# A last down projection with the tokens in rows: the final two token tiles of a decoder step on one Trainium2 core

## The reference

```
h2 = x * (1 + sc2) + sh2
ua, ub = jnp.split(h2 @ w_up, 2, axis=-1)
uc, ffn_conv_new = causal_dwconv(ua, ffn_conv_prev, w_ffn_conv, b_ffn_conv)
ffn = (jax.nn.gelu(uc) * ub) @ w_down
x = layer_norm(DN_ALPHA * x + g2 * ffn, ln2_g, ln2_b)
```

## Time and profile before

| | |
|---|---|
| median of 3 runs | 1551.62 us (1549.88 to 1554.25) |
| profiled execution, its own time | 1554.13 us |
| span of the profiled execution | 1552.5 us |
| TensorE busy | 1462.7 us (94%) |
| VectorE busy | 837.4 us (54%) |
| ScalarE busy | 404.1 us (26%) |
| GpSimd busy | 78.2 us (5%) |
| mean granted TensorE clock | 0.978 of full |

### The profile page before, as it was taken

How to read it: one execution, slowest core, us unless ns; L and a number is a source line. 1 busy time by engine, 2 the same in 40 slices (tenths; PEclk the granted TensorE clock), 3 DMA queues, 4 the chain that set the end, 5 groups by cost and what they waited for, 6 DMA issues and landing times.

```text
span 1552.5 us, 25588 instructions
## 1 busy us (share of the span) xinstructions
PE 1462.7 (94%) x9800; PEld 1312.1 (85%) x9800; DVE 837.4 (54%) x1273; ACT 404.1 (26%) x729; POOL 78.2 (5%) x111
## 2 busy tenths in 40 slices
PE   6999999799998999599899999999999999999996
PEld 3878787566565877499899999999999999999996
DVE  3306787994555564644754544445444454544566
ACT  2212434353544575624341210010000000010011
POOL 0333000000000000002210000000000000000013
PEclk9899999999999999899999999999999999999998
DMA  9865863763872111431211111111112111111122
GB/s 342 261 216 163 236 189 102 223 188 122 271 227 90 34 38 45 171 110 41 69 41 41 39 39 58 55 41 48 33 41 68 41 44 34 58 55 41 34 78 96
DMA packets 178111, 159.99 MB, mean 103 GB/s; under 512 B 12267, under 2 KB 158327, under 8 KB 178018
## 3 DMA queue, kind: packets, MB, share of 16 engines
q1 hardware_dynamic: 145412, 141.15, 28.7%
q10 hardware_dynamic: 30566, 17.50, 3.9%
q0 software_dynamic: 2048, 0.20, 0.2%
HBM read 142.25 MB, written 13.79 MB: 101 GB/s over the span
## 4 chain that ended last, share of the span: by engine, by line
PE 80%; DVE 10%; issue 3%; ACT 3%; SPq 2%; DMA 2%; ACTq 0%; DVEq 0%
PE ps L2185 43%; PE ps L1933 13%; PE ps L2136 5%; PE ps L2016 3%; PE ps L1994 3%; PE ps L2297 2%; PE ps L2034 2%; DVE stick L945 1%; PE ps L2048 1%; PE ps L1856 1%; DVE k_page L855 1%; PE ps L2236 1%; DVE pr L924 1%; SPq L610 1%; DVE pr L949 1%
## 5 line engine op out<-in xcount | busy, mean ns | idle before, releaser
L2185 PE MATMUL ps<-acts_lo,w_hi 128*128 128x344 f32 x1008 | 213.9, 320 | 0.0
L2185 PE MATMUL ps<-acts_hi,w_hi 128*128 128x344 f32 x1008 | 213.8, 320 | 0.0
L2185 PE MATMUL ps<-acts_hi,w_lo 128*128 128x344 f32 x1008 | 212.8, 319 | 0.0
L1933 PE MATMUL ps<-acts_hi,w_hi 128*128 128x344 f32 (+1 forms) x552 | 186.1, 337 | 6.5 <-DVE w_lo L813 2.9
L1160 DVE CAST w_hi<-w_raw 128x1024 fp32r<-128x1024 f32 x72 | 49.7, 690 | 239.4 <-PE ps L2185 227.7
L1933 PE MATMUL ps<-acts_lo,w_hi 128*128 128x344 f32 (+1 forms) x552 | 178.8, 324 | 0.0
L1933 PE MATMUL ps<-acts_hi,w_lo 128*128 128x344 f32 (+1 forms) x552 | 178.8, 324 | 0.0
L2185 PEld LDWEIGHTS ps<-acts_lo,w_hi 128*128 128x128 f32 x1008 | 170.6, 189 | 0.0
L2185 PEld LDWEIGHTS ps<-acts_hi,w_hi 128*128 128x128 f32 x1008 | 169.7, 188 | 0.0
L2185 PEld LDWEIGHTS ps<-acts_hi,w_lo 128*128 128x128 f32 x1008 | 167.9, 188 | 0.0
L1933 PEld LDWEIGHTS ps<-acts_hi,w_hi 128*128 128x128 f32 (+1 forms) x552 | 103.9, 188 | 24.1 <-issue 16.6
(11 more groups left out here) (334 smaller groups left out, 2398.1 us busy)
## 6 DMA issues: line engine op xcount, KB each, us to landing
w_ada<-in_w_ada SPq DMA_DIRECT2D x12, 2048.0 KB, 8.9
w_raw<-in_w_up SPq DMA_DIRECT2D x44, 512.0 KB, 3.8
k_page<-in_cache_fox_k SPq DMA_DIRECT2D x64, 192.0 KB, 3.0
k_page<-in_cache_sb_k SPq DMA_DIRECT2D x64, 192.0 KB, 2.9
k_page<-in_cache_fox_v SPq DMA_DIRECT2D x64, 192.0 KB, 2.9
k_page<-in_cache_sb_v SPq DMA_DIRECT2D x64, 192.0 KB, 3.6
w_raw<-in_w_in ACTq DMA_DIRECT2D x15, 512.0 KB, 5.5
w_raw<-in_w_down SPq DMA_DIRECT2D x16, 384.0 KB, 3.4
```

The source lines that it names most:

```text
L1933: last = nc.tensor.matmul(bank[0:cols, 0:CH], w[:, n % 2, k, 0:cols], a[:, k, c * CH:(c + 1) * CH], start=k == 0 and w is w_hi and a is ac ...
L2185: last = nc.tensor.matmul(proj_ps[half][:, c, 0:CH], w[:, half, k], a[:, k, c * CH:(c + 1) * CH], start=k == 0 and w is w_hi and a is hi, ...
```

## The change

Tiles 3 and 4 (n = 7, 8) no longer get their part of the last down projection with the features in partitions. In last_mms the tokens of the tile are the stationary operand (g_hi, g_lo: 128 x 128) and the weights the moving one, 512 columns wide, so that the product has the tokens in partitions and 512 features in columns; there are two halves for each tile, each of 5 x 3 products. No turn follows.

What this needs is made in the first span: side_rows turns, after m = 2, 4 and 6, the gate (one column of modT, repeated 128 times) into gate_rows, and resT of tiles 3 and 4, which lacks only the last group, into res_rows; ScalarE evicts all three (128 x 1024 each). ScalarE also copies the weights of the first two output tiles into the wide buffers wd_hi and wd_lo (four copies, w_c), since the moving operand is read from there.

In the new last_half VectorE multiplies the product by gate_rows, adds it to res_rows and takes the statistics of the half, in three instructions of 512 columns. norm_last now works on res_rows and writes the last instruction of tile 4 in two halves, each of which SyncE stores by itself.

The order on the engines is new: TensorE runs half 0 of tile 3, the turns of tiles 0 and 1, half 1 of tile 3, the turns of tile 2 and the two halves of tile 4. VectorE runs last_half(0, 0), norm2 of tiles 0 and 1, last_half(0, 1), norm2 of tile 2, norm_last(0), the two halves of tile 4 and norm_last(1). scale2 stays with VectorE for tiles 5, 6 and 7; for the sampled tokens and tiles 0, 1 and 2 GpSimd does the multiply by ln2g ahead of its addition of ln2b. SyncE stores tile 3 ahead of tile 2.

```diff
@@ gpsimd
-                pool.wait_ge(y_g, n + 1)
+                if n < Y_ROWS_DVE:
+                    pool.wait_ge(y_g, n + 1)
+                else:
+                    pool.wait_ge(y_n, n + 1)
+                    nc.gpsimd.tensor_tensor(y_tile[n % 3][0:rows], y_tile[n % 3][0:rows], ln2g[0:rows], ALU.mult).then_inc(y_g, 1)
+                    pool.wait_ge(y_g, n + 1)
                 nc.gpsimd.tensor_tensor(y_tile[n % 3][0:rows], y_tile[n % 3][0:rows], ln2b[0:rows], ALU.add).then_inc(y_o, 1)
@@ vector
+            def last_half(j, half):
+
+                dve.wait_ge(o_pm, D_AT + 2 * KT + 2 * j + half + 1)
+                at = Z_DONE * j + 3 * half
+                v = res_rows[:, j, half]
+                V.tensor_tensor(y_part[:], last_bank(j, half), gate_rows[:, half], ALU.mult).then_inc(z_d, 1)
+                dve.wait_ge(z_d, at + 1)
+                V.tensor_tensor(v, y_part[:], v, ALU.add).then_inc(z_d, 1)
+                dve.wait_ge(z_d, at + 2)
+                V.bn_stats(y_stat[:, j, 6 * half:6 * half + 6], v).then_inc(z_d, 1)
...
+                V.bn_aggr(st[:, 12:14], st[:, 0:12]).then_inc(y_d, 1)
                 dve.wait_ge(y_d, at + 1)
-                V.bn_aggr(st[:, 12:14], st[:, 0:12]).then_inc(y_d, 1)
-                dve.wait_ge(y_d, at + 2)
                 V.tensor_scalar(st[:, 14:15], st[:, 13:14], EPS, None, ALU.add).then_inc(y_d, 1)
...
+                V.scalar_tensor_tensor(out=y, in0=y, scalar=st[:, 12:13], in1=ln2g, op0=ALU.subtract, op1=ALU.mult).then_inc(z_g, 1)
+                dve.wait_ge(y_q, LAST_Y + j + 1)
                 V.reciprocal(st[:, 15:16], st[:, 14:15]).then_inc(y_d, 1)
...
+                for cols in ((slice(0, D),), (slice(0, 512), slice(512, D)))[j]:
+                    V.scalar_tensor_tensor(out=y[:, cols], in0=y[:, cols], scalar=st[:, 15:16], in1=ln2b[:, cols],
+                                           op0=ALU.mult, op1=ALU.add).then_inc(y_z, 1)
...
+            dve.wait_ge(r_e, 3)
+            last_half(0, 0)
+            norm2(at[0])
+            norm2(at[1])
+            last_half(0, 1)
+            norm2(at[2])
+            norm_last(0)
+            for half in range(2):
+                last_half(1, half)
+            norm_last(1)
@@ scalar
+            act.wait_ge(g_pm, G_DN0[-1] + 2)
+            for m in range(2):
+                act.wait_ge(g_ws, G_DN0[-1] + m + 3)
+                for wide, part in ((wd_hi, w_hi), (wd_lo, w_lo)):
+                    A.activation(wide[:, 0:GROUPS[-1], m * P:(m + 1) * P], part[:, m, 0:GROUPS[-1]], ACT.Copy).then_inc(w_c, 1)
             for c in range(3):
+                act.wait_ge(r_t, c + 1)
+                A.activation((gate_rows[:], res_rows[:, 0], res_rows[:, 1])[c], psB[:, 1:3], ACT.Copy).then_inc(r_e, 1)
@@ tensor
+            def side_rows(r):
+
+                pe.wait_ge(r_e, r)
+                for f in range(KT):
+                    if r == 0:
+                        side = modT[:, 5 * KT + f, 0:1].to_broadcast([P, P])
+                    else:
+                        side = resT[:, f, tok_cols(DTILES[2][r - 1])]
+                    last = nc.tensor.transpose(psB[:, 1 + f // 4, f % 4 * P:f % 4 * P + P], side, ident[:])
+                last.then_inc(r_t, 1)
+
+            def last_mms(j, half):
+
+                cols, n = slice(half * 512, half * 512 + 512), 2 * j + half
+                toks = tok_cols(DTILES[2][j])
+                pe.wait_ge(o_ev, D_AT + KT + 4 + n + 1)
+                for k in range(gs):
+                    for act, w in ((g_hi, wd_hi), (g_lo, wd_hi), (g_hi, wd_lo)):
+                        last = nc.tensor.matmul(last_bank(j, half), act[:, k, toks], w[:, k, cols],
+                                                start=k == 0 and w is wd_hi and act is g_hi, stop=k == gs - 1 and w is wd_lo)
+                last.then_inc(o_pm, 1)
...
+            pe.wait_ge(w_c, 4)
+            last_mms(0, 0)
+            pe.wait_ge(o_ev, D_AT + 2 * KT)
+            rows2(at[0])
+            rows2(at[1])
+            last_mms(0, 1)
+            rows2(at[2])
+            for half in range(2):
+                last_mms(1, half)
```

More of the change, by code:

```diff
@@ L222, in hybrid_step @@
         ffn_2 = sb9("ffn_2", [2 + NB, 2, 8, P])
+        gate_rows = sb9("gate_rows", [P, 2, 512])
+        res_rows = sb9("res_rows", [P, 2, 2, 512])
+        y_part = sb9("y_part", [P, 512])
+        y_stat = sb9("y_stat", [P, 2, 16])
         st9.close()
@@ L314, in hybrid_step @@
         y_f = sem("y_f")
+        y_l = sem("y_l")
+        r_t = sem("r_t")
+        r_e = sem("r_e")
+        w_c = sem("w_c")
+        z_d = sem("z_d")
+        z_g = sem("z_g")
         y_fs = sem("y_fs")
@@ L511, in hybrid_step, with last_bank @@
         ND, LAST_Y = len(DSPANS), len(DORDER) - 2
+        def last_bank(j, half):
+            return ((psA[:, 0], psB[:, 0]), (psA[:, 1], psA[:, 2]))[j][half]
+        Y_ROWS_DVE = len(DTILES[0]) - 1
+        Z_DONE = 6
         def tok_cols(tt):
@@ L1442, in norm_last @@
[L1442 to L1454, removed]
@@ L1455, in _ @@
-            for n in range(LAST_Y, len(DORDER)):
-                norm_last(n)
+                dve.wait_ge(y_d, at + 3)
+                dve.wait_ge(z_g, j + 1)
+                for cols in ((slice(0, D),), (slice(0, 512), slice(512, D)))[j]:
+                    V.scalar_tensor_tensor(out=y[:, cols], in0=y[:, cols], scalar=st[:, 15:16], in1=ln2b[:, cols],
+                                           op0=ALU.mult, op1=ALU.add).then_inc(y_z, 1)
+            at = [DAT[tt] for tt in DTILES[0]]
+            for m in range(KT):
+                down_add(1, m)
+                n = (m - 1) // 2
+                if m % 2 == 1 and n < len(at):
+                    norm2(at[n])
+                elif m % 2 == 0 and m and n < Y_ROWS_DVE:
+                    scale2(at[n])
@@ L1459, in _ @@
+            at = [DAT[tt] for tt in DTILES[1]]
+            dve.wait_ge(r_e, 3)
[8 more added lines that the diff above has]
+            norm_last(1)
         @block.scalar
@@ L1832, in _ @@
                              ACT.Copy).then_inc(y_f, 1)
-            for n, tt in enumerate(DORDER):
+            for n, tt in enumerate(DORDER[0:LAST_Y]):
                 rows = P if tt < TT else NB
-                roots(n, rows, y_d, y_q, 5 * n + 3 - max(0, n - LAST_Y))
-                if n >= LAST_Y:
-                    continue
+                roots(n, rows, y_d, y_q, 5 * n + 3)
                 if n >= 3:
@@ L1842, in _ @@
                              bias=ln_st[0:rows, n % 2, 14:15], scale=ln_st[0:rows, n % 2, 15:16]).then_inc(y_n, 1)
+            for j in range(2):
+                roots_last(j)
         @block.tensor
@@ L2332, in _ @@
                 down_project(0, m)
+                if m % 2 == 0:
+                    side_rows(m // 2 - 1)
                 if m in (3, 5, 7):
@@ L2339, in _ @@
                     last.then_inc(y_f, 1)
[L2340 to L2353, removed]
+            at = [DAT[tt] for tt in DTILES[0]]
+            for m in range(KT):
+                down_project(1, m)
+                if m == 1:
+                    pe.wait_ge(o_ev, D_AT + KT)
+                    pe.wait_ge(u_s, KT * len(GROUPS))
+                n = (m - 1) // 2
+                if m % 2 == 1 and n < len(at):
+                    rows2(at[n])
+            at = [DAT[tt] for tt in DTILES[1]]
+            pe.wait_ge(w_c, 4)
[5 more added lines that the diff above has]
+            rows2(at[2])
+            for half in range(2):
+                last_mms(1, half)
 _INS = ["x_prompt", "x_sample", "cache_fox_k", "cache_fox_v", "cache_fox_logf", "cache_sb_k", "cache_sb_v",
```

34 lines of the change are left out of this document (21 added, 13 removed).

## The result

| | before | after |
|---|---|---|
| median of 20 runs each, us | 1551.11 | 1556.84 |
| lowest to highest, us | 1546.69 to 1554.25 | 1551.64 to 1564.61 |
| ratio, 95% interval | | 1.0035 [1.0024, 1.0046] |
| profiled execution: time, span, us | 1554.13, 1552.5 | 1557.43, 1555.8 |
| end of VectorE's last instruction to the end of the span, us | 3.1 | 2.6 |

The change costs 5.4 us by the ratio (0.35% of 1551.11; the interval is 3.7 to 7.1 us). 1557.7 was predicted, and 1556.84 was measured.

What follows compares the result with a forecast made beforehand. From 1517.6 us VectorE's row was taken to bound the kernel. Undisturbed end 1545.0 plus 11.15 of holds gives 1556.1, 6.7 later; less 0.6 for the store, 6.1 more: 1557.7 us, range 1553.8 to 1560.5.

Steps and rivals of the forecast that it cites:

- Part 1: First span on TensorE: three added groups of eight turns delay what follows by 2.6 us; gate turn's possible extra 0.9 taken as 0.
- Part 2: Products of tiles 3 and 4: 512 columns take 0.232 us each, a half 3.56 us; nothing won in TensorE.
- Part 3: VectorE's row from 1524.0, if undisturbed: 21.0 us, ending at 1545.0, a win of 4.4 us.
- Part 4: Tail: GpSimd's added multiplies and adds hold VectorE's two-SBUF-input instructions at six places, 11.15 us, ending VectorE at 1556.1.
- TensorE's wait before tile 2: Third span: TensorE waits about 2.4 us before tile 2's turns; a clock fall there would not delay VectorE.
- Part 5: End of kernel: the last store is 256 KB instead of 512 KB and takes 0.65 us less.
- Sum: Whole tail: VectorE ends 6.7 us later, the last store saves 0.6, net 6.1 us more.
- Rival (a): VectorE beside GpSimd in the tail: no holding, span 4.0 us less, 1547.6 us; chance 0.12.
- Rival (b): VectorE's tail: only wide instructions are held, the one-column L1406 is not; median 1555.7 us; chance 0.22.
- Rival (c): bn_stats reading SBUF held too, or gate turn slow: 1 to 3 us more, 1559 to 1561; chance 0.07.

Runs made afterwards that it cites:

- e6_short_turns: Changed kernel with one turn of eight in each of the three side groups, the rest of those rows left out: 1557.01 us, ratio 1.0026 to before.
- e8_memset: Changed kernel with GpSimd's multiplies and additions of the last four row tiles replaced by memsets that only write: 1547.54 us, ratio 0.9979 to before.
- e2_one_sbuf_input: Changed kernel, all work kept, VectorE results written back to PSUM and the column instruction given a scalar operand: 1548.05 us, ratio 0.9976 to before.
- e10_half_stores: Kernel before with multiplies moved to GpSimd, no two-SBUF-input VectorE instructions after it, last tile finished and stored in halves: 1548.36 us, ratio 0.9971.
- e7_late_turn: Kernel of e2_one_sbuf_input with the turns of tile 4's residual moved from the first to the third span: 1547.36 us, ratio 0.9968 to before.
- e1_no_gpsimd: Changed kernel without GpSimd's multiply and addition for the last four row tiles, a 4-byte memset for each pair: 1547.38 us, ratio 0.9966 to before.
- e3_small_only: Changed kernel with only the one-column instruction L1434 changed, its second column now a scalar operand: 1556.32 us, ratio 1.0013 to before.

## Why the prediction was right, step by step

- **Part 1, 2.6 us of turns**: right. Counted from the mark at which the tail begins, the third span starts 2.65 us later (42.75 against 40.10), e6_short_turns took 7/8 of it back, and the gate turn cost 0.87 us like the others, so the bound of another 0.9 wasn't needed.
- **Part 2, the products**: right. TensorE's timeline shows them 0.233 us apart (0.232 was estimated), and a half takes 3.51 us (3.56).
- **Part 3, VectorE's row undisturbed, 21.0 us**: right, 21.1 us in e8_memset. It begins 46.6 us behind the mark there and in after; 1524.0 in the prediction is 46.5 behind it. But e8_memset leaves GpSimd's work out. With it, and without holds, the row is 21.7 (e2_one_sbuf_input).
- **Part 4, the holds**: the mechanism and the places were right, all six at the instructions that were named; the size was somewhat too large. They measure 1.59 (add (3,0)), 1.49 (column, tile 1), 1.67 (add (3,1)), 1.75 (column, tile 2), 1.89 (last instruction of norm_last, tile 3) and 1.43 (add (4,0)): 9.82 us for the 11.15 predicted. Each was walked as a full wait to GpSimd's end and then the whole instruction, but a held add ends 0.55 us behind GpSimd, not 0.69, the 1024-wide instruction 1.07 behind it, not 1.28, and a column 0.01 to 0.02, not 0.16. That makes 0.9 of the 1.3 us. The prediction had rows for it and did not use them: there a held instruction of 1.23 us ended 1.09 behind GpSimd's, and one of 0.23 ended 0.08 behind the earlier trace rows. The rest is in the moments of meeting, a few tenths off from those walked. The tail of e8_memset is 9.80 us shorter than that of after, the sum of the holds to 0.02.
- **TensorE's wait before tile 2**: 2.4 us were predicted, 2.20 measured. The fall of the clock that was allowed for came (below), and it cost nothing: the last product starts at 1538.90, and VectorE asks for the last two halves at 1544.47 and 1547.95.
- **Part 5, the last store**: 0.65 us less predicted, 0.54 measured (2.58 instead of 3.12 us behind VectorE's end); e10_half_stores shows the same on its own, from 3.2 to 2.6. It holds only while the store of tile 2 is long gone. Where the holds are removed and GpSimd's work is kept, it is not there: 3.14 us in e2_one_sbuf_input and 3.07 in e7_late_turn.
- **Sum**: VectorE's end was to come 6.7 us later and comes 5.69 later in the tail (77.54 us after its start instead of 71.85); less 0.54 that is the +5.15. The mis-sized term is the holds, 1.3 us too large, against 0.3 too much gain on the other terms.
- **The number came closer than its parts, in part by luck.** 6.1 us more were forecast, and the tail shows 5.15. Of the 0.9 us between 1557.7 and 1556.84, 0.5 is the base: the median of before is 1551.11 over 20 runs and was 1551.62 over the three that the prediction had. The profiled execution of after was to take 1560.2 and took 1557.43; 0.95 of these 2.8 us is the tail, and 1.85 is the stages ahead of the mark, which the change does not touch.
- **Rival (a)**, no holding, fell with the first add: 2.28 us, where it decided at 0.69. Its time is what e1_no_gpsimd, e8_memset and the operands in PSUM give, 1547.4 to 1548.1, close to the 1547.6 worked out for it; e2_one_sbuf_input also shows the crowded stores on which that number counted. **Rival (b)**, one column not held, fell with 1.65 and 1.91 us at L1434, and e3_small_only shows what a kernel of that kind does: 2.1 us less in the tail. **Rival (c)** fell with the bn_stats of 0.69 us inside a GpSimd instruction. That the measured median lies between the forecast and (b)'s 1555.7 is no support for (b).

## What to carry to other kernels

Before moving elementwise work to GpSimd, list what VectorE runs beside it: every VectorE instruction with two tensors in SBUF, one column wide or a thousand, may have to wait until a GpSimd instruction that reads SBUF has ended, and where VectorE sets the end that can outweigh the work moved (here 9.8 us of holds against 4.9 us of multiplies). If one operand can stay in PSUM, or come as a scalar operand, the same move wins: the tail went from +5.15 to -3.52 us with the new products, and from -1.92 to -4.36 with the old. Measure such a change by the stretch it touches, from a fixed mark to the end, since medians of the whole kernel scatter by more than the terms.

## What the runs showed of the hardware that was not expected

- **The clock fell sooner than in the kernel before.** TensorE's timeline of after, and its windows (length, busy PE, PEld, DVE, ACT, POOL, clock, DMA share, GB/s):

```profile
1527.02 0.40 PE L2402 MATMUL ps<-acts_lo,g_hi 128*128 128x512 f32 x1
1529.62 1.81 PE L2245 MATMUL ps<-ident,resT 128*128 128x128 f32 x8 [2.20 <-ACT w_raw L1891]
...
1531.66 0.63 PE L2402 MATMUL ps<-acts_hi,g_lo 128*128 128x512 f32 x1
```

```profile
1528.00:1529.00 1.00, 0.00 (x0) 0.00 (x0) 0.97 (x4) 0.63 (x1) 0.00 (x0) 1.00 0.23 33
1529.00:1530.00 1.00, 0.38 (x3) 0.38 (x4) 0.84 (x3) 0.63 (x2) 0.35 (x1) 0.92 0.00 0
1530.00:1531.00 1.00, 1.00 (x6) 1.00 (x5) 0.79 (x2) 0.14 (x1) 1.00 (x1) 0.50 0.00 0
...
1533.00:1534.00 1.00, 1.00 (x5) 0.83 (x4) 1.00 (x1) 0.33 (x1) 1.00 (x1) 0.87 0.03 8
```

  The last product starts at 1527.02, TensorE waits 2.20 us, and the granted clock is 0.92 in the slice from 1529 and at its lower level, 1.2 GHz, from 1530, when the turns already run; it is back at 2.4 GHz within the slice from 1533. In the kernel before it was still at 0.96 in the slice that begins 2.5 us after the last product's start. Eight turns took 1.81 us instead of 0.87. Beside a VectorE that is behind this costs nothing. On TensorE's path it would be nearly 2 us, by an estimate from these rows: 0.94 for the turns, and about as much again for the first products behind them, some of which start 0.43 us apart instead of 0.233. In e2_one_sbuf_input TensorE waits 0.69 us there, and the turns take 1.09.
- **A GpSimd instruction that only writes held nobody**: eight of 2.06 us in e8_memset, and VectorE's adds at 0.692 us.
- **Width makes no difference to being held**: one column of 128 rows took up to 1.91 us; the same product with its second factor as a scalar operand took 0.21 inside GpSimd's instruction, although that operand lies in SBUF too.
- **Neither does the number of rows on GpSimd's side**: its instruction on 8 rows lasts 2.35 us like that on 128, and holds VectorE as long.
